# Expert numbers of the chosen pairs read by exclusive or and minimum in place of one-hot, multiply and sum, with a short list for the first eight ranks

## What is computed

```python
q = (xt @ wq).reshape(TOKEN_BLOCK, PEER_HEADS, 2, half)        # 8 heads, two halves of 64
s1 = jnp.einsum('thd,hkd->thk', q[:, :, 0], key1)              # 128 scores of the first half
s2 = jnp.einsum('thd,hkd->thk', q[:, :, 1], key2)              # 128 of the second
v1, i1 = lax.top_k(s1, 16)
v2, i2 = lax.top_k(s2, 16)
comb = (v1[..., :, None] + v2[..., None, :]).reshape(TOKEN_BLOCK, PEER_HEADS, 256)
sc, pos = lax.top_k(comb, 16)
experts = take_along_axis(i1, pos // 16) * 128 + take_along_axis(i2, pos % 16)
gate = jax.nn.softmax(sc, axis=-1)
act = gelu(einsum('thkd,td->thk', u[experts], xt)) * gate      # 16384 experts u, v
out = einsum('thk,thkd->td', act, v[experts])
```

## Time and profile before

| | |
|---|---|
| median of three runs | 4504.73 us (4504.63 to 4519.54) |
| span of the profiled execution | 4504.3 us |
| TensorE busy | 4205.9 us (93%) |
| vector engine busy | 3126.5 us (69%) |
| ACT busy | 1558.1 us (35%) |
| GpSimd busy | 1504.4 us (33%) |

### The profile page before, as it was taken

How to read it: one execution, slowest core, us unless ns; L and a number is a source line. 1 busy time by engine, 2 the same in 40 slices (tenths; PEclk the granted TensorE clock), 3 DMA queues, 4 the chain that set the end, 5 groups by cost and what they waited for, 6 DMA issues and landing times.

```text
span 4504.3 us, 63924 instructions
## 1 busy us (share of the span) xinstructions
PE 4205.9 (93%) x22555; PEld 3573.1 (79%) x22555; DVE 3126.5 (69%) x6090; ACT 1558.1 (35%) x2721; POOL 1504.4 (33%) x1221
## 2 busy tenths in 40 slices
PE   7999999999899799989999999898798999999998
PEld 4668877777688578779889998898797888888886
DVE  7531037777477644459999788885467998888888
ACT  4221135556477533232222444442121222222222
POOL 0000000000044311003888788887853222222220
PEclk9999999999999899999999999999899999999999
DMA  6647323333456465233444699999898888888885
GB/s 263 244 168 248 127 84 128 114 126 121 155 175 203 133 214 186 85 110 88 83 80 94 156 264 264 265 274 275 219 338 303 299 307 288 286 288 285 286 289 196
DMA packets 479090, 913.42 MB, mean 203 GB/s; under 512 B 188675, under 2 KB 269971, under 8 KB 475269
## 3 DMA queue, kind: packets, MB, share of 16 engines
q1 hardware_dynamic: 321380, 509.42, 34.7%
q0 software_dynamic: 151136, 363.35, 27.0%
q10 hardware_dynamic: 6336, 37.75, 2.3%
HBM read 747.37 MB, written 188.17 MB: 208 GB/s over the span
## 4 chain that ended last, share of the span: by engine, by line
PE 26%; DVE 11%; POOL 10%; DMA 5%; issue 4%; SPq 1%; ACT 0%; DVEq 0%; ACTq 0%; POOLq 0%
PE ph_gate_ps L2482 15%; PE ph_hid_ps L2482 7%; POOL scratch_scattered L2357 5%; POOL ph_ring L2363 4%; DMA ph_ring<-in_u_rows,held_tiles 4%; PE ph_hid_ps L2407 3%; PE ph_hid_ps L2397 1%; DVE ph_hot L2669 1%; DVE ph_hot L2676 1%; DVE ph_ring L2781 1%; DVE ph_u_lo L2614 1%; DVE ph_score L2641 1%; DVE ph_index L2643 1%; DVE ph_index L2640 1%; DVE ph_placef L2679 1%
## 5 line engine op out<-in xcount | busy, mean ns | idle before, releaser
L2357 POOL DMA_INDIRECT scratch_scattered<-held_tiles x384 | 709.2, 1847 | 289.5 <-DVEq L2704 155.6
L2407 PE MATMUL ph_hid_ps<-ph_n_hi,ph_u_hi 128*128 128x384 f32 x2048 | 709.6, 346 | 67.8 <-DVE ph_u_lo L2614 67.8
L2407 PE MATMUL ph_hid_ps<-ph_n_lo,ph_u_hi 128*128 128x384 f32 x2048 | 700.2, 342 | 0.0
L2407 PE MATMUL ph_hid_ps<-ph_n_hi,ph_u_lo 128*128 128x384 f32 x2048 | 699.2, 341 | 0.0
L2383 POOL DMA_INDIRECT ph_ring<-in_v_experts,ph_pick_again x256 | 240.6, 940 | 778.4 <-DVE held_tiles L2887 743.4
L2781 DVE CUSTOM_DVE_ANT_0 ph_ring<-ph_ring,ph_n_rows 128x1024 f32<-128x1024 f32 x256 | 309.4, 1224 | 212.8 <-DMA ph_ring<-in_u_rows,held_tiles 212.0
L2407 PEld LDWEIGHTS ph_hid_ps<-ph_n_hi,ph_u_hi 128*128 128x128 f32 x2048 | 397.2, 194 | 75.5 <-DVE ph_u_lo L2614 75.2
L2407 PEld LDWEIGHTS ph_hid_ps<-ph_n_lo,ph_u_hi 128*128 128x128 f32 x2048 | 396.9, 194 | 0.2
L2407 PEld LDWEIGHTS ph_hid_ps<-ph_n_hi,ph_u_lo 128*128 128x128 f32 x2048 | 396.4, 194 | 0.0
L2363 POOL DMA_INDIRECT ph_ring<-in_u_rows,held_tiles x256 | 329.3, 1286 | 152.3 <-DVE held_tiles L2781 90.2
L2887 DVE SCALAR_TENSOR_TENSOR held_tiles<-ph_ring,ph_factor,held_tiles 128x1024 f32<-128x1024 f32 x254 | 324.7, 1278 | 0.0
(11 more groups left out here) (396 smaller groups left out, 9853.0 us busy)
## 6 DMA issues: line engine op xcount, KB each, us to landing
ph_u_raw<-in_tiles SPq DMA_DIRECT2D x136, 512.0 KB
ph_v_raw<-in_v_experts SPq DMA_DIRECT2D x124, 512.0 KB, 4.8
scratch_hidden<-ph_hidden SPq DMA_DIRECT2D x128, 384.0 KB, 4.3
ph_u_raw<-scratch_hidden SPq DMA_DIRECT2D x124, 384.0 KB, 4.9
proj_w_ch<-in_w_ch SPq DMA_DIRECT2D x49, 512.0 KB, 3.7
mb_w_raw<-in_w_branch POOLq DMA_DIRECT2D x48, 512.0 KB, 3.9
scratch_gate_tiles<-ph_gates SPq DMA_DIRECT2D x48, 512.0 KB
ph_hidden<-scratch_gate_tiles SPq DMA_DIRECT2D x124, 192.0 KB, 3.9
```

The lines of the kernel that those rows point to most:

```text
L2357: pool.indirect_dma_start(d["scattered"], bass.IndirectOffsetOnAxis(place_of[:, at:at + 1], 0), held[:, 2, GM + at:GM + at + 1], None, com ...
L2407: mm = pe.matmul(hid_halves[r][:, c, :], u[r][a][:, k, :], n2[b][:, k, c * CUT:(c + 1) * CUT], start=(k == 0 and a + b == 0), stop=(k == K ...
```

## The change

The ids carry the place of their pair. `make_pairs` adds to the first index's part of the id the place of the row's first pair, and to the second index its own number, both times 2^14 (`place_steps`, a new constant of 2 x 16 numbers). So the id of the pair at place p is p x 2^14 + expert number. `pair_id` is now uint32. A second list, `first_id`, holds the ids of only 20 pairs (`FIRST_ROWS`), which are all that can be among the best eight. `settle` shifts the places left by 14 bits in place of a conversion to float32. `place_differ` takes the exclusive or of a shifted place with every id of the list: it gives the bare expert number where the places agree and at least 2^14 elsewhere. `look_up` takes the minimum. The two parts of 64 picks are now not the first and last four token tiles but the first and last eight ranks of all eight; the first uses the list of 20 (1280 elements a partition), the second that of 50 (3200 elements).

```diff
--- before.py
+++ after.py
@@ -2017,6 +2017,9 @@

 PAIR_ROWS = [(0, 1, 16), (1, 2, 8), (2, 3, 5), (3, 4, 4), (4, 5, 3), (5, 8, 2), (8, 16, 1)]
 PAIRS = sum((a1 - a0) * nb for a0, a1, nb in PAIR_ROWS)
+FIRST_ROWS = [(0, 1, 8), (1, 2, 4), (2, 4, 2), (4, 8, 1)]
+FIRST_PAIRS = sum((a1 - a0) * nb for a0, a1, nb in FIRST_ROWS)
+PLACE_BITS = 14

@@ -2060,6 +2063,7 @@
     STEPS = GATE_TOK // PER_STEP
     SCATTERS = ST * TOPK
     HALF_PICKS = TT * TOPK // 2
+    RANKS = TOPK // 2
     d["hidden"] = nc.dram_tensor("scratch_hidden", (NK, P, SM), F32, kind="Internal").ap()
     d["gate_tiles"] = nc.dram_tensor("scratch_gate_tiles", (NK, NK, GM), F32, kind="Internal").ap()
     scattered_rows = d["scattered"].rearrange("(p e n) a -> p e (n a)", p=NK, e=NK)
@@ -2100,7 +2104,9 @@
             index = [topk_sb(f"index{s}", [P, TT, 2, TOPK], U32) for s in range(2)]
             indexf = [topk_sb(f"indexf{s}", [P, TT, 2, TOPK]) for s in range(2)]
             pair = [topk_sb(f"pair{s}", [P, TT, PAIRS]) for s in range(2)]
-            pair_id = [topk_sb(f"pair_id{s}", [P, TT, PAIRS]) for s in range(2)]
+            pair_id = [topk_sb(f"pair_id{s}", [P, TT, PAIRS], U32) for s in range(2)]
+            first_id = [topk_sb(f"first_id{s}", [P, TT, FIRST_PAIRS], U32) for s in range(2)]
+            place_steps = topk_sb("place_steps", [P, 2, TOPK])
             best = [topk_sb(f"best{s}", [P, TT, TOPK]) for s in range(2)]
             place = [topk_sb(f"place{s}", [P, TT, TOPK], U32) for s in range(2)]
             placef = [topk_sb(f"placef{s}", [P, TT, TOPK]) for s in range(2)]
@@ -2108,7 +2114,7 @@
             split_id = topk_sb("split_id", [P, DT, TOPK], I32)
             total = [topk_sb(f"total{s}", [P, TT]) for s in range(2)]
             waits = topk_sb("waits", [1, 10])
-            hot = topk_sb("hot", [P, HALF_PICKS, PAIRS])
+            differ = topk_sb("differ", [P, HALF_PICKS * PAIRS], U32)
             score_ps = first.enter_context(nc.psum_tensor("ph_score_ps", [P, TT, 2 * NK], F32))
         with ExitStack() as then:
             turn_ps = [then.enter_context(nc.psum_tensor(f"ph_turn_ps{b}", [P, HALF], F32)) for b in range(2)]
@@ -2251,6 +2257,7 @@
                 for g in range(GT):
                     sync.dma_start(n2_rows[:, g, :], d["n2_rows"][g]).then_inc(rows_in, 16)
                 sync.dma_start(token[:], d["token"]).then_inc(const_in, 16)
+                sync.dma_start(place_steps[:].rearrange("p a k -> p (a k)"), d["place_steps"].partition_broadcast(P)).then_inc(const_in, 16)
                 for r in range(2):
                     sync.sem_inc(hid_stored[r], 16)
                 load(2, 0, 1)
...
@@ -2645,11 +2652,14 @@
                 def make_pairs(s, own):
                     own.of(dve.tensor_copy(indexf[s][:], index[s][:]))
                     own.wait()
-                    own.of(dve.tensor_scalar(indexf[s][:, :, 0, :], indexf[s][:, :, 0, :], float(NK), None, ALU.mult))
+                    own.of(dve.scalar_tensor_tensor(indexf[s][:, :, 0, :], indexf[s][:, :, 0, :], float(NK),
+                                                    place_steps[:, 0, :].unsqueeze(1).to_broadcast([P, TT, TOPK]), ALU.mult, ALU.add))
+                    own.of(dve.tensor_tensor(indexf[s][:, :, 1, :], indexf[s][:, :, 1, :],
+                                             place_steps[:, 1, :].unsqueeze(1).to_broadcast([P, TT, TOPK]), ALU.add))
                     own.wait()
-                    for out, src in ((pair[s], top[s]), (pair_id[s], indexf[s])):
+                    for out, src, pair_rows in ((pair[s], top[s], PAIR_ROWS), (pair_id[s], indexf[s], PAIR_ROWS), (first_id[s], indexf[s], FIRST_ROWS)):
                         at = 0
-                        for a0, a1, nb in PAIR_ROWS:
+                        for a0, a1, nb in pair_rows:
                             na = a1 - a0
                             own.of(dve.tensor_tensor(out[:, :, at:at + na * nb].rearrange("p t (a b) -> p t a b", a=na),
                                                      src[:, :, 0, a0:a1].unsqueeze(3).to_broadcast([P, TT, na, nb]),
@@ -2658,25 +2668,29 @@
                     own.wait()

                 def settle(s, own):
-                    own.of(dve.tensor_copy(placef[s][:], place[s][:]))
+                    own.of(dve.tensor_scalar(place[s][:], place[s][:], PLACE_BITS, None, ALU.logical_shift_left))
                     own.of(dve.tensor_copy(total[s][:], best[s][:, :, 0:1].rearrange("p t a -> p (t a)")))
                     own.wait()
                     dve.tensor_tensor(best[s][:], best[s][:], total[s][:].unsqueeze(2).to_broadcast([P, TT, TOPK]),
                                       ALU.subtract).then_inc(place_ready, 1)

-                def place_hot(s, part, own):
-                    half = slice(part * HALF_PICKS, (part + 1) * HALF_PICKS)
-                    own.of(dve.tensor_tensor(hot[:], placef[s][:].rearrange("p t k -> p (t k)")[:, half].unsqueeze(2).to_broadcast(
-                        [P, HALF_PICKS, PAIRS]), iota[:, 0:PAIRS].unsqueeze(1).to_broadcast([P, HALF_PICKS, PAIRS]), ALU.is_equal))
+                def ranks_and_ids(s, part):
+
+                    ranks = slice(part * RANKS, (part + 1) * RANKS)
+                    ids, n = (pair_id[s], PAIRS) if part else (first_id[s], FIRST_PAIRS)
+                    return ranks, ids, n, differ[:, 0:HALF_PICKS * n].rearrange("p (t k n) -> p t k n", t=TT, k=RANKS)
+
+                def place_differ(s, part, own):
+
+                    ranks, ids, n, out = ranks_and_ids(s, part)
+                    own.of(dve.tensor_tensor(out, place[s][:, :, ranks].unsqueeze(3).to_broadcast([P, TT, RANKS, n]),
+                                             ids[:].unsqueeze(2).to_broadcast([P, TT, RANKS, n]), ALU.bitwise_xor))
                     own.wait()

                 def look_up(s, part, own):
-                    half = slice(part * HALF_PICKS, (part + 1) * HALF_PICKS)
-                    hot4 = hot[:].rearrange("p (t k) n -> p t k n", t=TT // 2)
-                    own.of(dve.tensor_tensor(hot4, hot4, pair_id[s][:, part * TT // 2:(part + 1) * TT // 2].unsqueeze(2).to_broadcast(
-                        [P, TT // 2, TOPK, PAIRS]), ALU.mult))
-                    own.wait()
-                    own.of(dve.reduce_sum(placef[s][:].rearrange("p t k -> p (t k)")[:, half], hot[:], AX.X))
+
+                    ranks, ids, n, out = ranks_and_ids(s, part)
+                    own.of(dve.tensor_reduce(placef[s][:, :, ranks], out, AX.X, ALU.min))
                     own.wait()

                 def weights_of(h, s, own):
...
@@ -2718,7 +2732,7 @@
                     split(0)
                     next(keyed)
                     if not first:
-                        place_hot(1 - s, 0, own)
+                        place_differ(1 - s, 0, own)
                     split(1)
                     if not first:
                         look_up(1 - s, 0, own)
...
@@ -2927,6 +2941,15 @@
     return out


+def place_steps():
+
+    first, at = [], 0
+    for a0, a1, nb in PAIR_ROWS:
+        first += [at + n * nb for n in range(a1 - a0)]
+        at += (a1 - a0) * nb
+    return np.array(first + list(range(TOPK)), np.float32) * np.float32(2 ** PLACE_BITS)
+
+
 def front_constants(a):

     b = np.arange(NB)
@@ -2965,7 +2988,7 @@
         "causal": np.where(n[None, :] <= n[:, None], 0, -1e30).astype(np.float32),
         "attn_norm_w": a["attn_norm_w"][0],
         "keysT": key_blocks(a["peer_key1"][0], a["peer_key2"][0]),
-        "iota": np.arange(NK, dtype=np.float32),
+        "iota": np.arange(NK, dtype=np.float32), "place_steps": place_steps(),
         "tiles": peer_tiles(a["peer_wq"][0].reshape(KD, P, PH, P).transpose(2, 1, 0, 3),
                             a["peer_u"][0].reshape(NK, NK, KD, P).transpose(1, 3, 2, 0)),
         "u_rows": a["peer_u"][0],
```

More of the change, by code:

```diff
@@ L2435, in _ @@
                     tile((1 + x) % 2, PERIOD // 2 * PH + (1 + x) // 2)
-                pe.wait_ge(const_in, 48)
+                pe.wait_ge(const_in, 64)
                 pe.wait_ge(head_done, PH)
@@ L2624, in _ @@
                 low(0, 1)
-                dve.wait_ge(const_in, 48)
+                dve.wait_ge(const_in, 64)
                 dve.wait_ge(n2_lo, KD + 1)
@@ L2704, in experts_of @@
                     dve.sem_inc(head_done, 1)
-                SELECT, COLLECT = 5 * 2 * TT + 5 + 2 + 2 * len(PAIR_ROWS) + 5 * TT + 5 + 2, 3 + 2 * 3 + 7
+                SELECT, COLLECT = 5 * 2 * TT + 5 + 3 + 2 * len(PAIR_ROWS) + len(FIRST_ROWS) + 5 * TT + 5 + 2, 3 + 2 * 2 + 7
                 def period(h, s, first, last):
@@ L2730, in period @@
                     if not first:
-                        place_hot(1 - s, 1, own)
+                        place_differ(1 - s, 1, own)
                     split(3)
@@ L2751, in _ @@
                     if x == 0:
-                        place_hot(1, 0, own)
+                        place_differ(1, 0, own)
                     if x == 1:
@@ L2756, in _ @@
```

(2 more changed lines are left out.)

## The result

| | before | after |
|---|---|---|
| median in the first comparison | 4504.68 us (4 runs) | 4458.18 us (4451.02 to 4466.94, 4 runs) |
| ratio | | 0.9891, 95% interval 0.9874 to 0.9909 |
| span of the profiled execution | 4504.3 us | 4449.4 us |
| same kernel again, five rounds | 4511.08 us | 4468.32 us, ratio 0.9906 (0.9889 to 0.9922) |
| a third time, five rounds | 4510.02 us | 4472.28 us, ratio 0.9914 (0.9900 to 0.9928) |

What follows compares the result with a forecast made beforehand. TensorE, waiting on the late vector engine, was taken to bound the kernel up to the first dot, GpSimd's queue afterwards. Span 4504.3 - 41 = 4463.3, plus 0.4 for the median: 4463.7, say 4464 us; range 4456 to 4486.

Steps and rivals of the forecast that it cites:

- TensorE's path: Head periods and thirteen tiles up to the first dot of a gathered row: TensorE through 41.1 us earlier.
- 28.0 us of waits: TensorE's eight waits for `ph_u_lo` in the seven head periods, caused by the late vector engine, would go.
- 13 of slow tiles: Rest of TensorE's 41.1 us: tiles that ran slowly behind those waits would lose 13 us.
- The vector engine holds it no longer: In each head period the vector engine's fifth split would come in time for TensorE, with 2.0 us of slack.
- The rival of the late engine: Vector engine still late for TensorE in the head periods: 4484 us if half the gain stays, 4478 if a third; 10%.
- GpSimd's path: Scatters up to head 4: starting 4.65 us earlier, 45 us less holding by two-input vector passes, head 4 near 2479.
- The stall at gather 4: GpSimd's wait for a ring slot freed by the first dot, 14.77 us before; forecast still there, some 20 us.
- The whole remainder shifts: From the first dot on, order of gathers, scatters, dots and tiles stays, so the rest moves rigidly by 41 us.
- GpSimd not freed: Rival: long scatters have another cause, so GpSimd's lane gains only 19.4 us, time 4485.3 us; 12%.
- Nothing arrives: Rival: the later stretch gives the gain back, for example by DMA traffic falling together differently; 4500 to 4505 us; 4%.
- Slower: Rival: uint32 passes on the vector engine run slower than forecast; at three times the price 4575 us; 4%.
- The last phase's row of 39 matmuls: Sign that the forecast is right: the last phase would start near 3419 us.

Runs made afterwards that it cites:

- late pass: Changed kernel plus an unused one-input minimum over 3200 elements a head, between the fourth and fifth split, behind the expert numbers; 4473.58 us.
- the pair of extra passes: Two kernels: changed kernel plus one unused 3200-element pass a head ahead of the third split, two-input exclusive or (4469.08 us) or one-input minimum (4466.44 us).

## Where the prediction was right, and which step failed

**TensorE's path: right, 1.9 us small.** Forecast 41.1 us less to the first dot, measured 519.6 - 476.6 = 43.0. A period took 2094.05 - 2037.75 = 56.30 in place of 56.47, 1.0 us less over six. The thirteen tiles took 2342.43 + 141.46 - 2037.75 - 6 x 56.30 = 108.3 in place of 109.2, 0.9 us less. The terms of 28.0 us of waits and 13 of slow tiles behind them were both real, since both went.

**The vector engine holds it no longer: right.** The net of 10 us a head came (82 us over eight), and only part of it was needed. The passes cost 1.49 and 3.49 us as forecast. The rival of the late engine fell with the waits, and the late pass shows how near it was.

**GpSimd's path: the mechanism right, the size wrong, without effect.** Two-input passes hold a scatter: the pair of extra passes shows it, but for the rival named there, the length of the result. I forecast a relief of 45 us and head 4 at 2479, and it was 72.4 - 36.5 = 35.9 and 2488.39. The passes themselves did as forecast. Put down to the vector instruction that ends 1.4 us ahead of the scatter's end, they held the scatters for 63.9 us before and 17.7 now, 46.2 us less. What I had put at nothing is that the scatters then meet other two-input instructions more often: `low` holds them for 15.3 us where it was 6.7, and the building of pairs and ids for 3.2 where it was 1.4. Counted in the order of time up to head 4, 31 scatters take 1.75 to 3 us where 18 did, and 7 more than 3 us where 28 did. The step asked for 23 us of relief, so it did not decide. The stall at gather 4 was 10.26 us, not 20.

**"The whole remainder shifts": the step that failed.** The prediction put at nothing by how much the rest of the execution moves by itself. Behind gather 4 thirteen profiles show 1935 to 1952 us, whatever the kernel. The forecast took this stretch as a constant, and the range's lower end left 8 us beyond the sum for everything. The first comparison's gain was 49.1 us: TensorE's path gave 1.9 of the 8 beyond the forecast. The other 6 can only be movement of whole executions, of this kernel's or of the one before, whose four times there go from 4501.51 to 4519.54; that they arose in this stretch is seen in one profile alone. The changed kernel's four times are 4451.02, 4452.22, 4464.15 and 4466.94, two pairs 12 us and more apart, and only the first was profiled. The first profile of the changed kernel is the shortest of the thirteen in this stretch, by 5.4 us, and it began period 1 earliest, 1.2 us before the first of before. With the 1.9 of TensorE's path that is 54.9 - 41.1 = 13.8 us: 1.2 + 1.9 + 10.7. Where in that stretch an execution differs is seen only roughly. From the first scatter of head 7 to gather 191 the first profile took 164.7 us and the others 170.6 to 178.5. The dots of the first profile also waited least of all for gathered rows, 207.9 us between 2500 and 3480, where the second profile of the same kernel has 219.2. Which of these is the cause stays open: no run varied it. That the stretch shifts as a whole is borne out by the repeats, whose 42 and 39 us stand beside the 43.0 of the path ahead of it.

**The rivals.** GpSimd not freed: fell, since its lane lost 35.9 us of holding. Nothing arrives: fell. Slower: fell with the passes' durations. The last phase's row of 39 matmuls, forecast near 3419, starts at 3406.04 in the first profile.

## What to carry to other kernels

An engine that waits for nothing can still be held: sum the durations of its instructions over the undisturbed one, and look at what another engine runs beside the long ones. Work out a saving per wait, and not per engine: the same pass of 3.5 us cost 0.7 us in all ahead of one split and 1.7 us a period ahead of another. When two lanes meet at one instruction, measure up to that instruction; here that distance repeats to 0.1 us where the stretch behind it moves by up to 13 in the same kernel, and a range must hold that movement as well. When a long pass that holds another engine is shortened, count what the other engine meets in its place.

## What the runs showed of the hardware

- GpSimd's scatter takes 1.55 us, and 3.37 and 4.44 where it starts under vector instructions with two inputs in SBUF. It then goes on about 1.42 us after such an instruction ends. A reduction of the same 3200 elements leaves it at 1.55, and so does a two-input pass that starts 0.29 us after it.
- Exclusive or and minimum over uint32 take the same time as comparison and sum over f32: 3.49 us for 3200 elements, 1.49 for 1280.
- Tiles behind a wait of TensorE can run slowly. The chain of before has query tiles of 13.97 and 12.99 us, each behind a wait for `ph_u_lo`, where the first of the stretch takes 11.25:

```profile
2039.08 11.25 PE ph_hid_ps L2397 x72
...
2221.34 13.97 PE ph_hid_ps L2397 x72
...
2346.36 12.99 PE ph_hid_ps L2397 x72
```

The windows of the head periods and the bridge say the same (stretch, its length, TensorE's busy time, then those of weight loads, vector engine, ACT and GpSimd, the granted clock as a share of 2.4 GHz, DMA share, GB/s), before and after:

```profile
2039.00:2528.00 489.00, 461.00 (x2595) 448.05 (x2594) 446.78 (x1787) 121.79 (x128) 370.02 (x192) 0.97 0.43 88
```

```profile
2039.00:2487.00 448.00, 446.43 (x2600) 438.07 (x2599) 363.92 (x1807) 123.57 (x132) 334.11 (x192) 1.00 0.46 97
```

The waits are 28 us of the 41 by which the stretch got shorter. The other 13 to 15 are TensorE's own busy time, 461.0 against 446.4 for the same work, with the granted clock at 0.97 before and 1.00 after. The 0.97 is a mean of the two levels. Before, seven stretches, some 31 us in all, are at 0.50, which is 1.2 GHz, and the rest at 2.4 GHz. One of them is the first half of the tile of 13.97 us:

```profile
2162.00:2219.00 57.00, 54.47 (x320) 53.07 (x319) 52.80 (x211) 15.53 (x16) 47.70 (x25) 1.00 0.41 80
2219.90:2226.50 6.60, 5.16 (x12) 4.10 (x13) 6.33 (x35) 0.00 (x0) 5.69 (x4) 0.50 0.75 139
```

Each of the seven begins during a wait of 1.8 to 4.9 us for `ph_u_lo` or at most 1.5 us after its end; the wait of 2.69 us has none behind it. Half of 31 us accounts for the 13 to 15 of busy time. The changed kernel has no such stretch between 2039 and 2487.
